# One buffer for the first two gate-up weight blocks, and a new order of the first two units, in a hybrid decoder block

## The reference

```
h = h + hybrid_mixer(rms_norm(h))          # gated DeltaNet beside causal pooling, gated merge
        merged = sigmoid(gate_a) * y_a + sigmoid(gate_b) * y_b;   return merged @ w_out
h = h + (silu(hn @ w_gate) * (hn @ w_up)) @ w_down                # hn = rms_norm(h); width 5632
h = rms_norm(h);  return h[:, 16:]
```

## Time and profile before

| what | value |
|---|---|
| median of 3 runs | 2702.34 us (2700.32 to 2702.71) |
| the profiled execution | 2702.11 us, its span 2700.2 us |
| TensorE busy | 2647.1 us (98%) |
| VectorE busy | 1838.7 us (68%) |
| ScalarE busy | 1002.7 us (37%) |
| mean DMA rate | 148 GB/s |

### The profile page before, as it was taken

How to read it: one execution, slowest core, us unless ns; L and a number is a source line. 1 busy time by engine, 2 the same in 40 slices (tenths; PEclk the granted TensorE clock), 3 DMA queues, 4 the chain that set the end, 5 groups by cost and what they waited for, 6 DMA issues and landing times.

```text
span 2700.2 us, 44485 instructions
## 1 busy us (share of the span) xinstructions
PE 2647.1 (98%) x17640; PEld 2419.3 (90%) x17640; DVE 1838.7 (68%) x1778; ACT 1002.7 (37%) x1029; POOL 343.3 (13%) x350
## 2 busy tenths in 40 slices
PE   8999999999999999999998999999999999999998
PEld 7999988888888987887878999999999998888886
DVE  4444545555554234548889888888888888888898
ACT  4443322222222232223344444444444444333334
POOL 5000044444442420110000000000000000000000
PEclk9999999999999999999999999999999999999999
DMA  4333222222223333679524445444544459866562
GB/s 138 101 88 90 79 79 79 84 79 78 78 78 87 107 95 116 221 258 329 187 94 144 150 158 174 152 151 148 179 148 158 152 168 308 287 207 203 175 196 105
DMA packets 345656, 398.75 MB, mean 148 GB/s; under 512 B 11481, under 2 KB 300386, under 8 KB 344418
## 3 DMA queue, kind: packets, MB, share of 16 engines
q1 hardware_dynamic: 285970, 333.30, 39.4%
q10 hardware_dynamic: 59616, 64.49, 7.0%
HBM read 325.92 MB, written 71.83 MB: 147 GB/s over the span
## 4 chain that ended last, share of the span: by engine, by line
PE 91%; DVE 3%; DMA 2%; issue 2%; ACT 1%; SPq 1%; POOL 1%; DVEq 0%; ACTq 0%; POOLq 0%
PE psum L2056 34%; PE psum L2373 10%; PE psum L2374 10%; PE psum L2375 10%; PE psum L2348 6%; PE psum L2350 6%; PE psum L2349 6%; PE psum L2216 2%; PE psum L2211 1%; PE psum L2005 1%; PE psum L2033 1%; DMA dn_raw<-in_w_ffn_down 1%; PE psum L2195 1%; DMA w_raw<-in_w_proj_a 1%; PE psum L2288 1%
## 5 line engine op out<-in xcount | busy, mean ns | idle before, releaser
L2056 PE MATMUL psum<-hn_hi,w_hi 128*128 128x264 f32 (+1 forms) x1600 | 450.5, 330 | 0.0
L2056 PE MATMUL psum<-hn_lo,w_hi 128*128 128x264 f32 (+1 forms) x1600 | 449.6, 330 | 0.0
L2056 PE MATMUL psum<-hn_hi,w_lo 128*128 128x264 f32 (+1 forms) x1600 | 449.5, 330 | 0.0
L1327 DVE TENSOR_TENSOR w_lo<-w_raw,w_hi 128x1024 fp32r<-128x1024 f32 x144 | 186.8, 1298 | 253.3 <-ACT w_hi L894 252.9
L894 ACT ACTIVATE w_hi<-w_raw 128x1024 fp32r<-128x1024 f32 x144 | 152.1, 1057 | 373.7 <-PE psum L2056 345.4
L2056 PEld LDWEIGHTS psum<-hn_lo,w_hi 128*128 128x128 f32 x1600 | 269.0, 188 | 22.6 <-issue 0.7
L2056 PEld LDWEIGHTS psum<-hn_hi,w_lo 128*128 128x128 f32 x1600 | 268.7, 188 | 22.5
L2056 PEld LDWEIGHTS psum<-hn_hi,w_hi 128*128 128x128 f32 x1600 | 269.0, 188 | 22.0 <-issue 0.2
L2348 PE MATMUL psum<-dn_hi,act_hl 128*128 128x512 f32 x616 | 240.7, 391 | 3.7 <-DVE dn_lo L1649 2.0
L2349 PE MATMUL psum<-dn_lo,act_hl 128*128 128x512 f32 x616 | 240.4, 390 | 0.0
L2350 PE MATMUL psum<-dn_hi,act_hl 128*128 128x512 f32 x616 | 240.2, 390 | 0.0
(11 more groups left out here) (355 smaller groups left out, 6394.3 us busy)
## 6 DMA issues: line engine op xcount, KB each, us to landing
w_raw<-in_w_in SPq DMA_DIRECT2D x144, 512.0 KB, 3.9
ffn_raw<-in_w_ffn_gate SPq DMA_DIRECT2D x44, 1024.0 KB, 6.5
ffn_raw<-in_w_ffn_up SPq DMA_DIRECT2D x44, 1024.0 KB, 6.5
dn_raw<-in_w_ffn_down SPq DMA_DIRECT2D x32, 1024.0 KB, 8.1
act_hl<-act_dram SPq DMA_DIRECT2D x56, 512.0 KB, 9.0
act_dram<-comb_hi ACTq DMA_DIRECT2D x22, 896.0 KB, 4.2
act_dram<-comb_lo ACTq DMA_DIRECT2D x22, 896.0 KB, 6.2
out_raw<-in_w_out SPq DMA_DIRECT2D x16, 1024.0 KB, 10.5
```

Of the source, the lines that this page charges most:

```text
L1327: dve.tensor_tensor(wlo[s][:], raw[s][:], whi[s][:].bitcast(F32), ALU.subtract).then_inc(S["lo_ready"], 1)
L2056: ins = pe.matmul(o, lhs, r, start=kt == 0 and i == 0, stop=kt == 4 * n_chunks - 1 and i == 2)
```

## The change

It has these parts.

1. `act_load(OUT, 0, "t4")` moves in SyncE's order from the `w_out` stage, behind the wait for `MG_STORED`, to the merge stage, behind the loads for b21 and t2 and ahead of the weight loads of merge units 6 and 7. Its buffer moves to `mixer_consts_at + 512`, and the four later `diag` tiles make room.
2. Gate-up blocks 0 and 1 both go through buffer `fraw[0]`; from then on gate blocks use `fraw[1]` and up blocks `fraw[0]`. Block 1 is loaded as soon as block 0's last low part (`low_c(0, 0)`) is formed; `low_c(0, 0)` moves forward to behind the first of the last two weighings. The `w_down` buffers are renamed to match.
3. For the last two token tiles ScalarE weighs quarters 1 and 3 (`weigh_act`: four 128x128 activations each), VectorE quarters 0 and 2.
4. TensorE runs A11 and A12 of unit 1 right behind S2 of unit 0, then S1, S3, S4, A22 of unit 0, then unit 1 from S2 on. `used(n, product)` recounts `chunk_used` for this. `split_a(0, 1)` and `low_a(0, 1)` move forward.
5. In the last unit `low_c` moves ahead of `c_11`.

```diff
-        diag += [place(f"diag{TT + 1 + i}", [P, P], at=mixer_consts_at + 6144 + 512 * i) for i in range(TT)]
+        diag += [place(f"diag{TT + 1 + i}", [P, P], at=(mixer_consts_at + 8704 if i < 2 else hn_at + 64 + 5 * 16384) + 512 * i)
+                 for i in range(TT)]
...
-        out_act_at = (raw_base + 8192, hn_at + 7168, hn_at + 7168 + 8192, wlo_at, wlo_at + 8192, qkv_at, qkv_at + 8192)
+        out_act_at = (raw_base + 8192, hn_at + 7168, hn_at + 7168 + 8192, wlo_at, wlo_at + 8192, qkv_at, mixer_consts_at + 512)
...
+        def fbuf(n, g):
+            return fraw[0] if isinstance(n, int) and n == 0 else fraw[1 - g]
...
-        dn_raw_at = (raw_base, raw_base + 8192, after_s, after_s + 8192, wlo_at + 8192, mixer_consts_at)
+        dn_raw_at = (after_s, after_s + 8192, raw_base, raw_base + 8192, wlo_at + 8192, mixer_consts_at)
...
+        def used(n, product):
+            early = isinstance(n, int) and n <= 1
+            moved = (2 if product > 3 else 0) if early and n == 0 else (-4 if product <= 2 else 0) if early else 0
+            return USED0 + 7 * n + product + moved
...
-                        sp.wait_ge(S["comb_stored"], MG_STORED)
-                        act_load(st, 0, "t4")
                         h_load(st, 1, (H_11, H_12, H_22, H_21))
...
             act_load(OUT, 0, "t2")
+            act_load(OUT, 0, "t4")
             with sp.Fori(early, N_MERGE) as u:
...
+            sp.wait_ge(S["lo_ready"], half_of(1, 3))
+            ffn_load(0, 1)
             sp.wait_ge(S["s_sum"], 4)
             sp.wait_ge(S["x_lo"], X0 // 2 + 4)
-            ffn_load(0, 1)
...
+            def weigh_act(t, q):
+                act.wait_ge(S["h_stored"], 32)
+                act.wait_ge(S["x_turned"], 4 * (TT + 1 + t) + q + 1)
+                for i in range(4):
+                    ins = act.activation(h_of(h, t, q)[:, P * i:P * (i + 1)], turn_bank(TT + 1 + t, q)[:, i, :], ACT.Copy,
+                                         scale=nffn[:, 4 * q + i:4 * q + i + 1])
+                ins.then_inc(S["x_weighed_a"], 1)
...
                 evict_p1(0, 0)
+                for c, t, kh in A_PIECES[4:6]:
+                    weigh_act(t, 1)
+                    weigh_act(t, 3)
+                    act.wait_ge(S["x_weighed_a"], 2 * (t - 2) + 2)
+                    act.wait_ge(S["x_weighted"], 4 * (TT + 3) + 2 * (t - 2) + 2)
+                    act.activation(s_piece(s_hi, c, t), y_piece(t, kh), ACT.Copy).then_inc(S["x_hi"], 1)
                 s_high(S1, s_sum[S1][:], 1)
                 s_high(S2, s_sum[S2][:], 2)
+                split_a(0, 1)
                 s_high(S4, s_sum[S4][:], 3)
-                for c, t, kh in A_PIECES[4:6]:
-                    act.activation(s_piece(s_hi, c, t), y_piece(t, kh), ACT.Copy).then_inc(S["x_hi"], 1)
                 s_high(S3, s_sum[S3][:], 4)
                 evict_u2(0, 0)
                 evict_q5(0, 0)
-                split_a(0, 1)
...
             low_b(0)
-            for t in range(2, TT):
-                weigh(t)
+            weigh(2)
+            dve.wait_ge(S["x_diag"], 2 * TT + 1)
+            low_c(0, 0)
+            low_piece(4)
+            weigh(3)
...
-            s_low(S2, s_sum[S2][:], 6)
+            s_low(S2, s_sum[S2][:], 8)
+            low_a(0, 1)
...
-            low_c(0, 0)
-            s_low(S4, s_sum[S4][:], 7)
-            dve.wait_ge(S["x_hi"], X0 + 9)
-            dve.tensor_tensor(by_tile(s_lo[A22]), y_half(1, 1), by_tile(s_hi[A22]).bitcast(F32), ALU.subtract) \
-                .then_inc(S["x_lo_v"], 1)
+            s_low(S4, s_sum[S4][:], 9)
+            low_piece(5)
...
                     begin()
+                    if last:
+                        low_c(n, g)
                     c_11(j, g)
-                    low_c(n, g)
...
-            unit_pe(0, 0, True, lambda: turn_h(range(2, TT)))
-            pe.wait_ge(S["x_weighted"], 4 * (2 * TT + 1))
-            unit_pe(0, 1)
+            head_pe(0, 0, True, lambda: turn_h(range(2, TT)))
+            second_pe(0, 0, True)
+            pe.wait_ge(S["x_weighted"], 4 * 2 * TT)
+            pe.wait_ge(S["x_weighed_a"], 4)
+            head_pe(0, 1)
+            rest_pe(0, 0, True)
+            second_pe(0, 1)
+            rest_pe(0, 1)
```

More of the change, by code:

```diff
@@ L1140, in split_a @@
                 else:
-                    act.wait_ge(S["chunk_used"], USED0 + 7 * n - 5)
-                act.activation(hi_a[:], fraw[g][:, :, 0:P], ACT.Copy).then_inc(S["hi_ready"], 1)
+                    act.wait_ge(S["chunk_used"], used(n - 1, 2))
+                act.activation(hi_a[:], fbuf(n, g)[:, :, 0:P], ACT.Copy).then_inc(S["hi_ready"], 1)
             def split_2(n):
                 act.wait_ge(S["t_done"], 3 * (n + 1) - 1)
-                after(act, "chunk_used", 7 * n - 4, USED0)
+                if not (isinstance(n, int) and n == 0):
+                    act.wait_ge(S["chunk_used"], used(n - 1, 3))
                 act.activation(two(hi_2s, n)[:], two(t2s, n)[:], ACT.Copy).then_inc(S["hi_ready"], 1)
@@ L1171, in evict_u2 @@
             def evict_u2(n, g):
-                act.wait_ge(S["chunk_used"], USED0 + 7 * n + 3)
+                act.wait_ge(S["chunk_used"], used(n, 3))
                 after(act, "c_done", 3 * n)
@@ L1177, in evict_q5 @@
             def evict_q5(n, g):
-                act.wait_ge(S["chunk_used"], USED0 + 7 * n + 4)
+                act.wait_ge(S["chunk_used"], used(n, 4))
                 act.wait_ge(S["c_done"], 3 * n + 1)
@@ L1753, in t_pair @@
                 else:
-                    dve.wait_ge(S["chunk_used"], USED0 + 7 * n - 2)
-                w = fraw[g][:]
+                    dve.wait_ge(S["chunk_used"], used(n - 1, 5))
+                w = fbuf(n, g)[:]
                 b12 = w[:, 0:HEADS, P:UNIT]
@@ L1764, in t_two @@
                 dve.wait_ge(S["t_done"], 3 * (n + 1) - 2)
-                after(dve, "chunk_used", 7 * n - 4, USED0)
-                dve.tensor_tensor(two(t2s, n)[:], t13[:, 0, :, :], fraw[g][:, HEADS:KT, P:UNIT], ALU.add).then_inc(S["t_done"], 1)
+                if not (isinstance(n, int) and n == 0):
+                    dve.wait_ge(S["chunk_used"], used(n - 1, 3))
+                dve.tensor_tensor(two(t2s, n)[:], t13[:, 0, :, :], fbuf(n, g)[:, HEADS:KT, P:UNIT], ALU.add).then_inc(S["t_done"], 1)
             def t_four(j, g):
@@ L1810, in weigh @@
                 dve.wait_ge(*((S["gates_stored"], STORED0 + 32) if t < 2 else (S["h_stored"], 32)))
-                for q in range(4):
+                for q in range(0, 4, 1 if t < 2 else 2):
                     dve.wait_ge(S["x_turned"], 4 * (TT + 1 + t) + q + 1)
@@ L1898, in unit_dve @@
                     begin()
+                    if last:
+                        low_c(n, g)
                     c_11(j, g)
-                    low_c(n, g)
-                if not last:
+                    if not last:
+                        low_c(n, g)
+                if last:
+                    next(begin_down)
+                elif not begun:
                     low_a(j + g, 1 - g)
-                else:
-                    next(begin_down)
                 beside()
-                dve.wait_ge(S["chunk_used"], USED0 + 7 * n + 5)
+                dve.wait_ge(S["chunk_used"], used(n, 5))
                 dve.wait_ge(S["evicted"], 3 * n + 3)
@@ L1911, in unit_dve @@
                     t_two(j + g, 1 - g)
-                dve.wait_ge(S["chunk_used"], USED0 + 7 * n + 6)
+                dve.wait_ge(S["chunk_used"], used(n, 6))
                 dve.wait_ge(S["evicted"], 3 * n + 2)
@@ L2363, in _ @@
             rows_products(OUT, lambda m, q: turn_h(range(2)) if m == OUT_UNITS - 1 and q == 5 else None)
-            S_DONE = {A11: ("x_lo", 3), A12: ("x_lo", 4), S2: ("x_lo_v", 1), S1: ("x_lo_v", 2), S3: ("x_lo_v", 3),
-                      S4: ("x_lo_v", 4), A22: ("x_lo_v", 5)}
+            S_DONE = {A11: ("x_lo", 3), A12: ("x_lo", 4), S2: ("x_lo_v", 2), S1: ("x_lo_v", 3), S3: ("x_lo_v", 4),
+                      S4: ("x_lo_v", 5), A22: ("x_lo_v", 6)}
             def product(c, w_hi, w_lo, k0, out, start, stop, first=False):
@@ L2379, in unit_pe, with unit_banks, head_pe @@
             def unit_pe(j, g, first=False, beside=lambda: None):
+                head_pe(j, g, first, beside)
+                second_pe(j, g, first)
+                rest_pe(j, g, first)
+            def unit_banks(g):
+                return (PS[:, 3 * g + i, 0:UNIT] for i in range(3))
+            def head_pe(j, g, first=False, beside=lambda: None):
                 n = 2 * j + g
-                a, b, c = (PS[:, 3 * g + i, 0:UNIT] for i in range(3))
+                a, b, c = unit_banks(g)
                 pe.wait_ge(S["lo_ready"], half_of(n + 1, 0))
@@ L2388, in unit_pe, with second_pe @@
                 product(A12, hi_a, lo_a, HEADS, b, True, True, first)
+            def second_pe(j, g, first=False):
+                n = 2 * j + g
+                a, b, c = unit_banks(g)
                 pe.wait_ge(S["lo_ready"], half_of(n + 1, 1))
```

(3 more changed lines are left out.)

36 lines of the change are left out of this document (20 added, 16 removed).

## The result

| | before | after |
|---|---|---|
| median of 20 runs each | 2700.89 us | 2705.34 us |
| lowest to highest | 2697.81 to 2705.28 | 2700.41 to 2708.17 |
| profiled execution | 2702.11 us | 2700.7 us |

The ratio is 1.0018, 95% interval 1.0012 to 1.0024: 4.4 us slower by the medians, inside the 5.4 us that I called no change, near its edge. I forecast 2703.4 us, a change of +1.1 us. The total is in the range, but the change is a quarter of the measured one, and two terms behind it are too small. Luck helped the total: my base, the median of three runs, was 2702.34 us, 1.5 us above the median of twenty.

The account below looks back on a forecast made before the run. TensorE, working 98% of the span, bounds the kernel. -5.2 + 5.0 + 1.6 - 0.3 = +1.1 us on the profiled 2702.11 us gives 2703.2, with the median 0.2 above: 2703.4 us, range 2696.5 to 2708.5.

Parts of the forecast that it names:

- the 5.4 us that I called no change: Whole kernel: about 0.2% can't be told from none; faster means under 2696.9 us, slower over 2707.7.
- Part 1, the w_out stage: -5.2: At t4 in w_out: the wait for `out_act` goes, saving 3.5 us idle and 1.7 us of slow clock.
- the rival that loads take it back: w_out stage: TensorE waits for a weight block or the residual instead; gain lost whole gives 2708.6 us; chance 0.17.
- Part 1, the merge stage: +5.0: Merge unit 6: first weight chunk 5.4 us late, TensorE idle 3.35 us for `gate_a`, plus 1.7 us of slow clock.
- The rival that the merge stage absorbs the load: Merge stage: first chunk at most 3 us late, stall 0 to 1 us, total 2699.0 us; chance 0.3.
- Parts 2 to 4: +1.6: Transition: waits before S4 and A22 go, but unit 1's S2 waits 2.5 us for `evict_p1`, then 1.5 us slow clock.
- Part 5: -0.3: Start of w_down: loads issued 2.4 us earlier into a full queue hardly land earlier; bounds -2.4 and +1.7 us.
- My bounds for the merge term: Merge unit 6: cost between +1.0 us (added bytes at full queue rate) and +6 us (all of the store first).
- slower than 2707.7: Slower outcome, chance 0.16, mostly from the w_out gain not being kept, with more than 4.1 of 5.2 us lost.

Follow-up runs that it names:

- experiment 9: The kernel before again, no edit, for a second profile: 2699.15 us against 2699.70, ratio 0.9999.
- experiment 2: Changed kernel with t4's load behind the weight loads of merge units 6 and 7: 2700.77 us against 2700.57 for the kernel before, ratio 1.0005.
- experiment 4: Changed kernel with t4's load behind those weight loads and only unit 1's A11 moved: 2694.36 us against 2700.57 for the kernel before, ratio 0.9983.
- experiment 5: Kernel before with part 1 alone, t4's load ahead of merge units 6 and 7: 2702.16 us against 2700.76, ratio 1.0005.
- experiment 11: Changed kernel with one of t4's two DMAs ahead of merge units 6 and 7, the other behind their weights: 2702.42 us, ratio to before 1.0011.
- experiment 1: The changed kernel again, no edit, for a second profile: 2705.44 us against 2700.57 for the kernel before, ratio 1.0020.
- Experiment 3: Changed kernel with only unit 1's A11 moved, A12 behind unit 0's A22 as before: 2700.47 us against 2700.57 for the kernel before, ratio 1.0000.
- experiment 10: Kernel before with t4's load alone moved, between the weight loads of merge units 6 and 7: 2696.64 us against 2699.70, ratio 0.9991.
- experiment 12: Changed kernel with part 1 undone, t4's load at its old place: 2702.89 us against 2699.56 for the kernel before, ratio 1.0013.

## Why the prediction was right, and where it was off

**Part 1, the w_out stage: -5.2.** Right. No wait, no slow matmuls; from the first matmul of merge unit 6 to A11 of unit 0 before takes 212.7 us and after 208.0, -4.7, and beside the second profile of before, whose stretch is 1.0 us shorter, -3.7. The wait that it removes is itself not constant, 2.5 us in the second profile of before (experiment 9) and 3.5 in the first. The gain was kept: the rival that loads take it back did not happen, except that with t4's load behind (experiments 2, 4) 1.4 to 1.5 us came back at 1255 us.

**Part 1, the merge stage: +5.0.** Right in mechanism, too small. Place (unit 6), releaser (`gate_a`), cause (two more DMAs ahead of the first chunk in SyncE's queue) are as said, and experiments 2, 5 and 11 show them; that the queue has half of the engines is in the rows of the queues. From the mark to unit 6's first matmul it is 16.1 us before, 19.5 to 21.6 in the six profiles with t4 ahead: 3.5 to 5.5 us later, where I had 3.35. To that come 2.0 to 2.6 us of slow clock in four of six: behind the wait 209.9 to 210.5 us instead of 208.0. The term is 3.5 to 7.5. I took the chunk's delay from the landing distance of two chunks at the half rate, 5.4 us, and in the profile of after it is 5.5. In the profile of experiment 1 it is 7.6 us. What I left out is SyncE's own time at the issue: the weight loads are issued 0.6 us behind the mark before, 4.7 in after and 6.0 in experiment 1, because SyncE takes 6.33 and 7.66 us for the six `out_act` DMAs. That the queue is full and holds SyncE is my reading; no run shows it. The rival that the merge stage absorbs the load is refuted.

**Parts 2 to 4: +1.6.** Each step came as said: the first sum 0.57 us later (said 0.55), the waits before S4 and A22 gone, 2.58 us of idle (said 2.5) released by `evict_p1`, slow matmuls behind it. From C_22 to `evict_p1(1)` it is 7.68 us, before 7.67: the chain kept its length, as said. The sum is right in three of six profiles with this order (+1.4 to +1.7), and +3.1 to +3.4 in the other three. There S2 of unit 0 takes 5.26 us until the next starts, where it takes 4.4 to 4.6 in the first three, and the products behind it are spaced wider (below). I had taken one value, 4.4 us, for a time that differs by 0.9 from one execution to the next. Experiment 3 shows which product made the new wait: A12.

**Part 5: -0.3.** Nothing measurable. The first wait there is 1.8 us in every profile with part 5 and 2.0 to 2.3 without; the one behind it is 0.8 to 2.7 us with it and 0.5 to 2.6 without, so what is gained at the first is lost in the spread of the second. The step behind it came as said: SyncE issues the `w_down` loads 2.3 us earlier from unit 2 on (said 2.4), and VectorE's `t3` sum starts at the same distance, 800.7 us behind unit 2's first matmul in both kernels.

**The whole.** -4.7, then 3.5 to 7.5, then 1.4 to 3.4 add up to 0.2 to 6.2 us, around the 4.4 measured (1.2 to 7.2 with -3.7). My bounds for the merge term ended at +6 and for the transition at +2.5: both should have reached higher, because I took the chunk's delay, the slow clock and S2's length at the size of one profile. One sum of the prediction is off by a little: slower than 2707.7 needs 4.3 us of the 5.2 lost, not 4.1.

**What stays open.** With t4's load behind or between in the changed kernel, the first chunk comes 13.1 to 14.0 us behind the mark; in the kernel before (twice), in experiment 10 and in experiment 12 it is 10.7 to 11.1, at about the same bytes moved; SyncE takes 3.0 to 3.3 us for the four `out_act` DMAs ahead of it in the first group and 2.2 to 2.4 in the second. Neither the new place of the load (experiment 10) nor parts 2 to 5 (experiment 12) do it alone; why the two together do is open. Nor do I know why the transition has two lengths.

## What to carry to other kernels

A load that TensorE waits for late in one stage may not move ahead for nothing: look at which load then stands behind it in the same queue, and how much slack its reader has. Here the place behind the loads of unit 6, which were urgent, and ahead of those of unit 7 cost least. When products are moved forward to fill a wait, count what they covered where they stood, and move only as many as the wait can take; here one of two was worth 5 us. And where several stalls of 2 to 5 us are weighed against each other, take a second profile before the sum is believed.

## What the hardware showed that I had not expected

**Two spacings at the full clock.** In the windows 1428 to 1440 us the same kind of matmul (128x256) starts 104 times in after and 108 times in the kernel with part 5 undone, TensorE busy all the time and the granted clock 1.00 in both:

```profile
1428.00:1440.00 12.00, 12.00 (x104) 12.00 (x103) 7.11 (x6) 0.39 (x1) 0.00 (x0) 1.00 0.30 101
```

```profile
1428.00:1440.00 12.00, 12.00 (x108) 12.00 (x107) 8.65 (x7) 2.54 (x3) 0.00 (x0) 1.00 0.56 176
```

By the starts it is 0.118 us against 0.113. The wider spacing lasts some 10 to 40 us, begins behind a wait or behind slow matmuls, ends in the middle of work, and costs 0.2 us for each 48 matmuls (5.65 us instead of 5.44). It is in both profiles of before too (1439 to 1450 us in the first). What sets it is open.

**Slow clock is not decided by the length of the idle time alone.** 3.3 and 3.5 us for `gate_a` left the clock up, 3.7 us did not. But 2.5 us ahead of t4 brought it down (experiment 9), 2.6 to 2.8 us in the transition always did, and so did 1.97 us at the start of the w_down stage of before, where the next matmuls are 0.43 us apart. 2.9 us at 1255 us brought it down in one profile and 2.8 us did not in another.

**A part of a queue's cost is paid at the issue.** SyncE took 2.2 to 3.3 us for four DMAs and 6.3 to 7.7 us for six, 1.5 to 2.7 us for each of the last two: what stands behind is late by that before its transfer begins.
